# Long convolution of a hybrid conv/Conformer block: from 2 phases (16 channels x 8 shifts, four 512-token matmuls) to 4 phases (8 channels x 16 shifts, three 256-token matmuls)

## What is computed

```python
h = rmsnorm(x, norm_g) * (1 + scale) + shift          # scale, shift, gate: from the conditioning vector
a_in, a_b, a_c, a_z, b_v, b_g, b_z = split(h @ w_in)  # 7 blocks of 512 channels
y_a = a_b * dwconv3(a_c * a_in) * silu(a_z)
u   = b_v * sigmoid(b_g)
u   = dwconv31(u) + conv_b_b                          # the long convolution: 31 taps, each channel by itself
y_b = silu(head_layernorm(u)) * silu(b_z)             # mean and variance over groups of 64 channels
y   = concat(y_a, y_b) @ w_out
out = rmsnorm(x + gate * y, final_g)
```

## Time and profile before

| | us |
|---|---|
| median of 3 runs | 2233.69 (2232.13 to 2260.23) |
| profiled execution | 2235.12 |
| its span, slowest core (3) | 2233.5 |
| its span, fastest core (6) | 2220.0 |
| TensorE busy on core 3 | 2165.8 |
| VectorE / ScalarE / GpSimd busy | 1326.2 / 980.0 / 628.2 |

### The profile page before, as it was taken

The page is one execution under the profiler, slowest core; times in us unless marked ns, Lnnn a source line. Parts: engine busy times, 40 slices in busy tenths (PEclk is TensorE's granted clock), DMA queues, the critical chain, the costliest instruction groups (busy, mean ns, idle before and its releaser), DMA issues.

```text
span 2233.5 us, 38878 instructions; the slowest of 8 cores (2220.0 to 2233.5 us)
## 1 busy us (share of the span) xinstructions
PE 2165.8 (97%) x11524; PEld 963.5 (43%) x11524; DVE 1326.2 (59%) x2251; ACT 980.0 (44%) x1644; POOL 628.2 (28%) x564
## 2 busy tenths in 40 slices
PE   4998999999999999999999999999999999999997
PEld 1443444444444444444444444444444444444443
DVE  1245574656657556476655747566575665647578
ACT  2232626345263443535435263443626445263464
POOL 3223324223242331423313242131311312122123
PEclk9999999999999999999999999999999999999999
DMA  9977477786766878668676777567565766656666
GB/s 259 155 212 192 131 186 197 201 199 183 190 188 197 212 183 175 174 191 236 180 202 175 195 229 209 153 185 171 168 187 154 195 196 155 187 128 204 159 180 223
DMA packets 300314, 418.49 MB, mean 187 GB/s; under 512 B 168616, under 2 KB 225104, under 8 KB 291920
## 3 DMA queue, kind: packets, MB, share of 16 engines
q1 hardware_dynamic: 291712, 408.50, 68.0%
q0 software_dynamic: 7392, 7.34, 2.6%
q10 hardware_dynamic: 1008, 0.17, 0.0%
HBM read 265.43 MB, written 92.82 MB: 160 GB/s over the span
## 4 chain that ended last, share of the span: by engine, by line
PE 88%; DMA 6%; DVE 2%; issue 1%; SPq 1%; ACT 1%; POOL 0%; DVEq 0%; POOLq 0%; ACTq 0%
PE pb L525 64%; PE pb L757 19%; PE pb L648 4%; DMA xb<-w_out 3%; DMA u_scratch<-u 1%; DMA V<-w_ada 1%; DMA w_in_sb<-w_in 1%; DVE sq L663 1%; SPq L393 0%; ACT sq L656 0%; PE pb L671 0%; PE pb L689 0%; DVE hT L386 0%; SPq L345 0%; DVE xb L810 0%
## 5 line engine op out<-in xcount | busy, mean ns | idle before, releaser
L525 PE MATMUL pb<-hT,w_in_sb 128*128 128x512 bf16 x7168 | 1578.5, 380 | 16.6 <-DMA w_in_sb<-w_in 9.7
L525 PEld LDWEIGHTS pb<-hT,w_in_sb 128*128 128x128 bf16 x7168 | 699.3, 98 | 875.9 <-issue 46.6
L531 ACT ACTIVATE tp<-pb 128x512 f32<-128x512 f32 x384 | 227.0, 595 | 618.3 <-PE pb L525 566.8
L768 DVE TENSOR_TENSOR xb<-pb,xb 128x512 f32<-128x512 f32 x252 | 171.4, 689 | 197.2 <-PE pb L757 185.3
L786 ACT ACTIVATE tp<-xb 128x1024 bf16<-128x1024 f32 x126 | 133.4, 1059 | 314.0 <-DVE xb L768 218.6
L757 PE MATMUL pb<-w_out_sb,yB 128*128 128x512 bf16 x960 | 251.2, 379 | 4.5
L757 PE MATMUL pb<-w_out_sb,yA 128*128 128x512 bf16 x960 | 246.3, 379 | 3.0 <-DVE xb L768 1.9
L797 POOL TENSOR_TENSOR rsE<-msE,mhalf 128x1 f32<-128x1 f32 x128 | 139.5, 1090 | 385.8 <-DVE msE L795 368.4
L324 POOL TENSOR_TENSOR rsA<-msA,mhalf 128x2 f32<-128x2 f32 x64 | 46.2, 722 | 649.9 <-DVE msA L322 649.9
L605 DVE SCALAR_TENSOR_TENSOR tp<-t,caT_sb,tp 128x512 f32<-128x512 bf16 x256 | 195.3, 763 | 28.4 <-DVE tp L602 1.4
L534 DVE TENSOR_TENSOR t<-pb,tp 128x512 bf16<-128x512 f32 x128 | 88.3, 690 | 160.7 <-PE pb L525 116.2
(11 more groups left out here) (102 smaller groups left out, 1308.2 us busy)
## 6 DMA issues: line engine op xcount, KB each, us to landing
xb<-x SPq DMA_DIRECT2D x254, 512.0 KB, 7.9
V<-u_scratch SPq DMA_DIRECT2D x128, 527.5 KB, 9.0
y<-xb SPq DMA_DIRECT2D x126, 512.0 KB, 3.9
xb<-w_out SPq DMA_DIRECT2D x40, 512.0 KB, 12.8
YP<-gst SPq DMA_DIRECT2D x64, 256.0 KB, 5.0
yB<-YP SPq DMA_DIRECT2D x120, 128.0 KB, 3.0
u_scratch<-u SPq DMA_DIRECT2D x80, 130.0 KB, 3.6
wg_scratch<-xb SPq DMA_DIRECT2D x32, 256.0 KB, 9.5
```

The lines of the kernel that those rows point to most:

```text
L525: T.op("tensor", lambda e, bank=bank, kc=kc: e.matmul(bank[:], lhsT=w_in_sb[:, kc, col0:col0 + 128], rhs=hT2[q][:, kc, :], start=(kc == 0) ...
L531: T.op("scalar", lambda e: e.activation(out=t[:], in_=bank[:], func=func, scale=scale), reads=[bkey], writes=[tkey])
L768: T.op("vector", lambda e, bank=bank, xbuf=xbuf, h=h: e.tensor_tensor(out=xbuf[:, h * NT:(h + 1) * NT], in0=bank[:], in1=xbuf[:, h * NT:(h ...
```

## The change

The split goes from 2 phases to 4 (NP = 4, tokens 4m + r, NB = 256 of each). A half q now holds the phases q and q + 2, side by side as 2 x 256 columns, so that the projections keep their 512 columns. `V` holds 4 residues x 8 channels x 4 shifts. A unit of 64 channels needs 2 x 4 groups (h, g) of 8 channels and 3 steps a of 16 taps, with 256 tokens each: 24 matmuls of half the length in place of 16. The means and variances become products with 256 columns, since the two halves of a unit's bank belong to the same tokens; `add4` therefore has a fourth, shorter add, and `ln_center` and the SiLU of `ln_fin` are two instructions of 256 columns per unit. `conv_quad` issues the matmuls of all four units and then the four copies, without the bias (it goes into `cbc` once, by `center_bias`). `vread` is four DMAs of 32 rows in place of two of 64, `y_move` eight per quad in place of four, and `g_move` eight in place of two and on ScalarE's queue. A window with neighbours on both sides stores its halo in two DMAs in place of one. Mixer A's 3-tap convolution `conv_a` has two full and two half instructions in place of three full ones. `TP` has 4 buffers in place of 6; the mean and the inverse deviation have a ring `MR` of their own (2 buffers). The ring of `u` has 3 in place of 4.

The second quad's convolution moves from slot 15 to 14, and the norm steps move as `norm_hooks` shows.

```diff
-        UR = Ring("u", [sb("u%d" % i, [128, VW], BF16) for i in range(4)], T)
+        UR = Ring("u", [sb("u%d" % i, [128, 2, VW], BF16) for i in range(3)], T)
-        TP = Ring("tp", [sb("tp%d" % i, [128, NT], F32) for i in range(6)], T)
+        TP = Ring("tp", [sb("tp%d" % i, [128, NT], F32) for i in range(4)], T)
+        MR = Ring("mr", [sb("mr%d" % i, [128, NB], F32) for i in range(2)], T)
...
+                for k, (ww, c, m) in enumerate(sides):
+                    T.dma("sync", lambda e, ww=ww, c=c, m=m: e.dma_start(out=u_rows(ww, q, j, c, PAD), in_=ub[:, :, m:m + PAD]),
+                          reads=[ukey], writes=[("Uh", q, j, w, ww)], semkey=("uh", ww > w) + ukey)
...
         def g_move(q):
-            T._need("sync", T._deps("sync", [], VK["YP"]))
-            for h in range(2):
-                T.dma("sync", lambda e, h=h: e.dma_start(out=YP[q::2, h::2, :], in_=gst[64 * h:64 * h + 64, :, :]),
-                      reads=GSK, writes=[("yp", u, q) for u in range(h, 8, 2)], semkey=("gm", q, h))
+            T._need("scalar", T._deps("scalar", [], VK["YP"]))
+            for u in range(8):
+                T.dma("scalar", lambda e, u=u: e.dma_start(out=YP[q::2, u, :], in_=gst[32 * (u % 4):32 * (u % 4) + 32, 2 * (u // 4):2 * (u // 4) + 2, :]),
+                      reads=GSK, writes=[("yp", u, q)], semkey=("gm", q, u))
...
+            for b in range(4):
+                k = b
+                src = U_d[p, j]
+                src = bass.AP(src.tensor, src.offset + k, [[VN, 32], [1, VN - k]])
+                T.dma("sync", lambda e, b=b, k=k, src=src: e.dma_start(
+                    out=buf[32 * b:32 * b + 32, :, :].rearrange("p g t -> p (g t)")[:, 0:VN - k], in_=src),
+                    reads=deps, writes=[(key, b)], semkey=("vl", key, b))
...
+        def conv_quad(p, hh):
...
+            for u, h, a, g in itertools.product(us, range(2), range(3), range(4)):
...
+                T.op("tensor", lambda e, vb=vb, bank=bank, g=g, h=h, a=a, j=j, G=G: e.matmul(
+                    bank[32 * g:32 * g + 32, NB * h:NB * h + NB], lhsT=WC[:, 64 * a + 16 * j + G, :], rhs=vb[:, G * VW + 4 * a:G * VW + 4 * a + NB],
+                    start=(a == 0), stop=(a == 2), tile_position=(0, 32 * g)),
+                    reads=[("WC", 2 * a + j // 2)] + vkeys, writes=[bkey], signal=(a == 2 and h == 1 and g == 3))
...
+            for u in us:
+                bank, bkey = cst[u]
+                vv, vvkey = sqr.next(pin=True)
+                T.op("scalar", lambda e, bank=bank, vv=vv: e.activation(out=vv[:], in_=bank[:], func=AF.Copy), reads=[bkey], writes=[vvkey])
...
         def add4(us):
             a, b, c, d = [cst[u][2:] for u in us]
             for (x, xk), (y, yk) in ((a, b), (c, d), (a, c)):
                 T.op("vector", lambda e, x=x, y=y: e.tensor_tensor(out=x[:], in0=x[:], in1=y[:], op=ALU.add), reads=[xk, yk], writes=[xk])
+            x, xk = a
+            for n in (NB,):
+                T.op("vector", lambda e, n=n: e.tensor_tensor(out=x[:, 0:n], in0=x[:, 0:n], in1=x[:, n:2 * n], op=ALU.add), reads=[xk], writes=[xk])
...
         def norm_hooks(hh, h, mid, post):
             add(mid, h + 1, lambda: add4(quad(hh)))
-            add(mid, h + 2, lambda: conv_mean(hh))
-            add(mid, h + 2, lambda: ln_center(hh))
-            add(mid, h + 3, lambda: add4(quad(hh)))
-            add(mid, h + 4, lambda: ln_var(hh), lambda: ln_act(hh))
-            add(mid, h + 5, lambda: fin2(hh, 0))
-            add(post, h + 5, lambda: fin2(hh, 1))
+            add(post if hh else mid, h + 2, lambda: conv_mean(hh), lambda: ln_center(hh))
+            add(mid, h + 4, lambda: add4(quad(hh)))
+            add(post if hh else mid, h + 5, lambda: ln_var(hh), lambda: ln_act(hh))
+            if hh:
+                add(mid, h + 6, lambda: fin2(hh, 0))
+                add(post, h + 6, lambda: fin2(hh, 1))
+            else:
+                add(post, h + 5, lambda: fin2(hh, 0), lambda: fin2(hh, 1))
...
-            for hh, h in enumerate((9, 15)):
-                add(post, h, lambda hh=hh: conv4(p, hh))
+            for hh, h in enumerate((9, 14)):
+                add(post, h, lambda hh=hh: conv_quad(p, hh))
...
-                add(post, h + 6, lambda hh=hh: y_move(hh, yb))
+                add(mid, h + 7, lambda hh=hh: y_move(quad(hh)[:2], yb))
+                add(post, h + 7, lambda hh=hh: y_move(quad(hh)[2:], yb))
```

More of the change, by code:

```diff
@@ L1 @@
 import contextlib
+import itertools
 import numpy as np
@@ L20 @@
 SEQ_WINS = (8, 2, 2, 2, 2)
-PAD = 8
-VW = NT + 2 * PAD
-VN = 8 * VW
+NP = 4
+NB = 256
+PAD = 4
+VW = NB + 2 * PAD
+VN = 16 * VW
 class Tracker:
@@ L642, in conv_b @@
[L642 to L658 removed]
+            deps = []
@@ L670, in conv_mean @@
             mb, mbk = PB.next()
[L671 to L673 removed]
+            T.op("tensor", lambda e: e.matmul(mb[:, 0:NB], lhsT=Bn[:], rhs=vv[:, 0:NB], start=True, stop=True), reads=["Bn", vvkey], writes=[mbk])
+            m, mkey = MR.next(pin=True)
+            T.op("scalar", lambda e: e.activation(out=m[:], in_=mb[:, 0:NB], func=AF.Copy), reads=[mbk], writes=[mkey])
             cst[("m", hh)] = (m, mkey)
@@ L822, in seq @@
             return run
-        def conv4(p, hh):
-            for u in quad(hh):
-                conv_b(p, u)
         def fin2(hh, i):
@@ L1056, in period0 @@
             add(post, 8, build_conv_w)
+            add(post, 13, center_bias)
             add(post, 9, lambda: T.dma("sync", lambda e: e.dma_start(out=fg_bc[:], in_=fg_d.partition_broadcast(128)),
```

346 lines of the change are left out of this document (176 added, 170 removed).

## The result

The changed kernel takes **2318.6 us** (median of 3 runs, 2315.5 to 2321.3) against 2233.7: ratio 1.034, 95% interval 1.022 to 1.046. It is slower, by 85 us where I had forecast 11 us less. In the profiled execution the slowest core is 2, with 2316.8 us, 83.3 more than core 3 before; the fastest takes 2287.4.

What follows compares the result with a forecast made beforehand. TensorE bounds the kernel, through its instruction times and whether the norm chain is ready for its mean. 2235.1 - 33.7 - 9.7 - 3.4 + 7 + 19 + 1.5 + 4 + 3 = 2222.8 us; range 2194 to 2247.

Steps and rivals of the forecast that it cites:

- TensorE's own work: TensorE's convolution quads and mean and variance matmuls: 0.109 us a step, saving 26.9 and 6.8 us, -33.7 in sum.
- rival C: Convolution on TensorE: weight loads not hidden in 256-token steps, 77 us more, total 2300; chance 0.05.
- The waits for the mean: TensorE before the second quad's mean: 1.0 us in 7 windows, 2.4 in 8 with the side job, replacing 9.7.
- a bound of 3.4: Upper limit of a side-job window's wait at the mean, in us, with one more add held when weights arrive late.
- rival B: Second quad's mean: the new waits don't come, as the last adds start before GpSimd's `pre_mul`; 2198 us, chance 0.25.
- the reads of V: Second quad's convolution: its second block of `V` may land late; 1.5 us for the sum of windows.
- Rival D: Second quad: `V` lands 5 us later in 8 side-job windows, costing 19 us and 6 of half clock; 2248, chance 0.17.
- The clock term: TensorE's half clock after waits over 2 us: -3.4 us for two old ones, +4 for two or three new.
- The ends: Start and end of the kernel: `center_bias`, larger `WC` and the last window together, +3 us (-2 to 8).
- the last window's shorter cover: Last window: less work to cover its waits, counted within the +3 us for both ends of the kernel.
- What I had at nothing: `y_move`, `g_move`, `conv_a` and `TP` in the windows: no cost, with 0.7 us to spare for `yB`.
- my three conditions for being wrong: On TensorE: a step over 0.12 us, waits for `V` in more than two windows, or the mean's input ready.

Runs made afterwards that it cites:

- Experiment 3: Changed kernel with the second quad's slot and the norm steps put back as in the kernel before: 2323.5 us, ratio 1.040.
- 12: Changed kernel with the scaling of w_out on VectorE in place of GpSimd, one slot later: 2304.3 us, ratio 1.032.
- 13: Kernel before with the scaling of w_out on VectorE in place of GpSimd, one slot later: 2226.6 us, ratio 0.998.
- experiment 9: Kernel before with one halo store for each side in place of one for both, 256 packets of 16 bytes in two stores: 2234.0 us, ratio 1.001.
- Experiment 1: Changed kernel without its halo stores, so tokens at window edges are wrong: 2269.5 us, ratio 1.015.
- experiment 8: Kernel before with its halo in twice as many, half as long pieces (8 bytes), same bytes: 2265.3 us, ratio 1.014.
- 14: Changed kernel with the side job (loading, scaling and storing w_out for later sequences) in windows 7 to 14 in place of 2 to 9: 2311.5 us, ratio 1.035.
- experiment 11: Changed kernel with its halo stores issued on ScalarE's queue in place of SyncE's: 2323.2 us, ratio 1.038.

## Why the prediction was wrong

**TensorE's own work** was right in kind. A quad lasts 1631.78 - 1629.03 = 2.75 us to the next projection, 0.115 a step, and up to 2.87 (0.120) elsewhere; I had 0.109. A window without its waits is 1.63 us shorter (132.27 - 1.05 against 133.15 - 0.30), where I had 2.1: 26 us in all in place of 33.7. The loads are hidden; rival C is out, though its 2300 lies nearest to the time that was measured.

**The waits for the mean** came where I said. Without the side job 0.53 us (0.3 to 0.4 forecast), and a window is 132.3 us long (132.05). With it 3 us in five windows and 0.8 in one, against 1.8: the adds ended 14.5 us after the variance began, not 13.2, because GpSimd's earlier multiply was late for its weights and pushed the `YP` multiplies and the next `pre_mul` back by 1.4 us. I had named this case as a bound of 3.4. In the other two windows the first quad's variance waited in its place (1.4 and 0.7 us). The sum for the mean, 17 us beside the side job, is near the 14 in my terms (8 x 1.8); rival B is out. But I took the shorter time for what makes the adds meet GpSimd's multiply. Experiment 3 shows that the old distances do not remove the waits, while 12 and 13 show that taking this multiply off GpSimd does.

**The step that failed is the reads of V**: "I count 1.5 us for the sum of windows", and before it "Halving the DMAs changes no bytes". In place of 1.5 us TensorE waited 48.4 us for `V` on the slowest core (33.7 on average; 41.0 with all waits at the convolution), and much of the half clock follows these waits. I asked only when the second pair of reads lands after its issue. I did not ask what the first pair waits for ahead of its issue: the stores of `u` and its halo. Before, its second block landed only 0.4 to 2.5 us ahead of the quad in most windows, and is needed 1.8 us into it. That margin was in the trace and not in my rows. And I counted the doubled halo stores nowhere: neither as issues (which would have been right: experiment 9) nor as packets. Experiment 1 takes them away and gets 43 to 49 us back, experiment 8 puts them into the kernel before and costs it 32.

**Rival D** had the direction, with 0.17, and the wrong mechanism. It put the lateness on SyncE's issues and on the second quad, 19 us. Issues cost nothing that can be told (9), the side job alone makes 0.4 to 2.1 us a window (14), and of the 48.4 us 44.7 are at the first quad.

**The clock term** (+4 net of -3.4) was too small because it hung on the waits. Waits over 2.5 us are mostly followed by half clock, as I had read from two; behind 200 us there are sixteen of them on the slowest core, and over the whole span 33 us more are lost than before.

**The ends** (+3, bound 8) measured 9.6 + 7.3. At the start VectorE stood 8.6 us before its fourth `u`, since the ring has three buffers and the stores queue behind the weight loads; the hT of the second half came 7.7 us late by that. I had not priced the ring of `u` at all. The last window's mean waits 4.9 us; I had put "the last window's shorter cover" into the 3.

**What I had at nothing** (`y_move`, `g_move`, `conv_a`, `TP`) cost next to nothing in the full windows: one wait for `yB` of 0.4 us stands there on the slowest core (up to 1.1 on others). Of my three conditions for being wrong one came true, `V` in more than two windows; a step of 0.120 us is at the edge of another.

## What to carry to other kernels

When a change regroups data, count the packets and their bytes on every transfer, small ones above all, and not only bytes and issues: eight halo stores of 4 KB in each of six windows, cut into twice as many pieces of half the length, cost the kernel before 32 us, and other transfers take longer beside them. For each transfer that is read just in time, take from the trace its margin (need less landing) over all windows, and follow the chain one step further back, to what its issue waits for. And where an add is late beside another engine's long instruction, more time before it may not help; moving the long instruction does.

## What the runs showed of the hardware

- DMA engines can be busy and move little: share 0.87 at 65 GB/s with the halo in 512 pieces of 8 bytes per store of `u`, 0.39 at 123 GB/s with none, in the same 14 us of one window; over six windows and all cores 0.67 at 114 against 0.41 at 127. Twice the packets of 16 bytes cost the kernel before 13 us, twice as many of 8 bytes 29 (both against experiment 9). The Trainium skill (DMA: Bandwidth & Descriptors, Specifications) gives 512 bytes as the least size for full rate and a read-modify-write below it. That small packets cost agrees; that those of 8 bytes cost more than those of 16 is these runs' own.
- Small packets delay what runs beside them: 512-byte packets of `u` took 56 ns on average with them and 30 without. It makes no difference which engine issues them (experiment 11).
- Reads of 528 bytes brought `V` later than reads of 8448, by longer issues (7.5 us for eight in place of 4.4) and by slower landings (1.7 us apart in place of 1.4): the second block 1 to 2.5 us after the quad's start, where long reads without a halo (experiment 1) end 0.1 to 2.2 us ahead of it in eleven of fifteen windows.
- Two bf16 adds took 0.96 us alone and 3.38 beside GpSimd's multiplies, the last one of 2.5 us; each ended 0.28 us after the multiply that it met. On VectorE this last multiply takes 1.22 us.
- Half clock: 5 stretches on the slowest core before, 18 after, mostly at or behind a wait of TensorE of over 2.5 us; before, one followed a wait of 2.2.
